# A decoder layer with an expert gather on one core: a new order ahead of the first gather, a planned share of the sums, and the gate multiply moved to ScalarE

## The reference, cut to what matters

```python
z = x @ w_in                      # split into [pool | q | k | v | gate_pool | gate_attn]
m = sigmoid(g_pool) * (pool_out @ w_up_pool) + sigmoid(g_attn) * (attn_out @ w_up_attn)
x = layer_norm(ALPHA * x + m @ w_out)                       # layer norm 1
def peer(xb):                                               # a block of 128 tokens
    q = (xb @ w_query).reshape(128, 8, 2, 128)
    sc = einsum('thcd,hcnd->thcn', q, sub_keys)             # 8 heads, two halves, 128 keys each
    ...                                                     # product-key top 16 of 128*128 experts
    gate = softmax(best_s)                                  # [128, 8, 16]
    u = take(expert_u, idx); h = gelu(einsum('td,thkd->thk', xb, u))
    return einsum('thk,thkd->td', gate * h, take(expert_v, idx))
x = layer_norm(ALPHA * x + peer(x))                         # layer norm 2
```

## Time and profile before

| | us |
|---|---|
| median of 3 runs | 3237.91 (3232.53 to 3238.44) |
| the profiled execution | 3230.01 |
| its span, from the first to the last instruction | 3228.2 |
| TensorE clock granted, mean | 0.929 of full |
| busy: PE / DVE / ACT / POOL | 2623.8 / 2404.6 / 687.4 / 1262.6 |
| DMA | 1258.54 MB, mean 390 GB/s |

### The profile page before, as it was taken

How to read it: one execution, slowest core, us unless ns; L and a number is a source line. 1 busy time by engine, 2 the same in 40 slices (tenths; PEclk the granted TensorE clock), 3 DMA queues, 4 the chain that set the end, 5 groups by cost and what they waited for, 6 DMA issues and landing times.

```text
span 3228.2 us, 28882 instructions
## 1 busy us (share of the span) xinstructions
PE 2623.8 (81%) x7884; PEld 1407.8 (44%) x7884; DVE 2404.6 (74%) x5540; ACT 687.4 (21%) x2001; POOL 1262.6 (39%) x1060
## 2 busy tenths in 40 slices
PE   8789999889898978889889898988666667666766
PEld 7776566555454534444344454443222222222222
DVE  2178666999967667898887667788999996666666
ACT  2123312222231121221332112221211121111111
POOL 0022343334443433334334343433445445444543
PEclk9899999999999989999999999999888888888898
DMA  6899999999999989999999999999999999999997
GB/s 200 234 385 368 354 412 386 408 368 406 413 420 416 420 358 414 420 399 413 358 348 379 419 420 405 408 405 383 376 418 419 420 382 422 421 421 422 421 422 330
DMA packets 204215, 1258.54 MB, mean 390 GB/s; under 512 B 31132, under 2 KB 34796, under 8 KB 68496
## 3 DMA queue, kind: packets, MB, share of 16 engines
q0 software_dynamic: 152064, 1107.36, 84.3%
q1 hardware_dynamic: 49376, 143.45, 12.2%
q10 hardware_dynamic: 2616, 5.88, 0.5%
HBM read 1250.93 MB, written 5.79 MB: 389 GB/s over the span
## 4 chain that ended last, share of the span: by engine, by line
PE 39%; DVE 26%; DMA 23%; issue 4%; DVEq 3%; ACT 3%; POOL 1%; SPq 0%; ACTq 0%; POOLq 0%
DMA ring<-in_uv,idx 21%; PE acc L890 20%; PE wide L873 11%; DVE ring L1139 10%; DVEq L1125 3%; DVE acc_v L1149 3%; PE wide L1047 3%; PE wide L1069 2%; ACT diag L689 1%; DMA wring<-in_w_q 1%; DVE hw L1144 1%; PE wide L981 1%; PE wide L963 1%; DVE ipart L1456 1%; DVE big L1448 1%
## 5 line engine op out<-in xcount | busy, mean ns | idle before, releaser
L890 PE MATMUL acc<-ring,diag 128*128 128x512 f32 (+1 forms) x3168 | 1637.2, 662 | 547.0 <-ACT diag L689 546.3
L652 POOL DMA_INDIRECT ring<-in_uv,idx x1056 | 1262.4, 1195 | 1939.1 <-PE acc L890 1558.6
L1139 DVE CUSTOM_DVE_ANT_0 ring<-ring,xb 128x1024 f32<-128x1024 f32 x1056 | 1269.7, 1223 | 356.4 <-DMA ring<-in_uv,idx 354.9
L890 PEld LDWEIGHTS acc<-ring,diag 128*128 128x128 f32 (+1 forms) x3168 | 631.5, 208 | 1411.7 <-issue 1391.8
L873 PE MATMUL wide<-xm,wring 128*128 128x256 f32 (+5 forms) x2624 | 638.0, 394 | 20.5 <-DMA wring<-in_w_q 16.5
L873 PEld LDWEIGHTS wide<-xm,wring 128*128 128x128 f32 x2624 | 462.1, 195 | 219.7 <-issue 98.0
L679 ACT ACTIVATE hgelu<-hdot 128x2 f32<-128x2 f32 x528 | 107.1, 203 | 1453.5 <-DVE hdot L1139 1452.9
L689 ACT ACTIVATE diag<-ident,hw 128x128 f32<-128x128 f32 x768 | 279.2, 395 | 539.6 <-DVE hw L1144 539.1
L1149 DVE SCALAR_TENSOR_TENSOR acc_v<-ring,hw,acc_v 128x1024 f32<-128x1024 f32 x264 | 339.3, 1285 | 27.0 <-issue 2.6
L1144 DVE TENSOR_TENSOR hw<-hgelu,gate 128x2 f32<-128x2 f32 x528 | 85.0, 161 | 122.3 <-ACT hgelu L679 104.4
L1069 PE MATMUL wide<-wring,big 128*128 128x256 f32 (+1 forms) x576 | 131.1, 380 | 1.1 <-DVE big L1332 1.1
(11 more groups left out here) (190 smaller groups left out, 1265.4 us busy)
## 6 DMA issues: line engine op xcount, KB each, us to landing
wring<-in_w_a SPq DMA_DIRECT2D x168, 512.0 KB, 7.7
wring<-in_w_q SPq DMA_DIRECT2D x64, 576.0 KB, 8.2
ring<-in_uv,idx POOLq DMA_INDIRECT x1056, 12.6
xb<-in_x_rows SPq DMA_DIRECT2D x8, 512.0 KB, 12.6
out_y_prompt<-xb ACTq DMA_DIRECT2D x8, 512.0 KB, 8.3
att<-in_ln_g SPq DMA_DIRECT2D x4, 512.0 KB, 8.2
att<-in_ln_b SPq DMA_DIRECT2D x4, 512.0 KB, 11.6
xm<-in_xT SPq DMA_DIRECT2D x1, 1536.0 KB, 11.5
```

Source lines behind the costliest of these rows:

```text
L652: pool.indirect_dma_start(ring[:, s % RING, :], None, uv, bass.IndirectOffsetOnAxis(ap=idx[:, n % ROWS, j:j + 1], axis=0))\
L890: k = mm(acc[0:width, c * 512:(c + 1) * 512], diag[:, r % DIAGS, 0:width], ring[:, s % RING, D + c * 512:D + (c + 1) * 512], start=(s == f ...
L1139: V.tensor_tensor_reduce(u, u, x, 1.0, 0.0, ALU.mult, ALU.add, hdot[:, k, j:j + 1])\
```

## The change

There are three parts.

1. **The order in front of the first gather, and some places in the other groups.** `store_states()` is called after the load of gate unit 6 instead of after the last unit of `w_out`. The pool mixer's product of group 0 goes to other PSUM banks (`mix_banks`) and stands after the twelfth gate unit. The sample attention's last product stands behind `w_out`. The first unit of `w_out` waits for half the merged channels only. The table `FIRST_ATTENTION` has other numbers. In groups 1 to 3 some ACT evacuations stand 0.3 to 0.5 of a batch later, and group 1's plan ends 3 batches earlier.
2. **The table of sums.** `ON_DVE`, before the second slot of every second batch, comes from `plan_sums()`, which adds up estimated costs of PE and DVE for each batch and gives a batch's second slot to DVE where its estimate says so. Summed by DVE in each of the nine peer parts, in order of time (the sixth is the samples): before 32, 32, 32, 32, 32, 8, 32, 32, 32, in all 264; now 42, 15, 33, 25, 48, 7, 1, 24, 31, in all 226. PE sums the rest, 792 before and 830 now. In the second part the first 40 batches give DVE none.
3. **The gate multiply.** DVE's `tensor_tensor` on `hw` is gone. ACT multiplies each slot's gelu by its gate with one ACTIVATE (a copy scaled by a column of `gate`) for each slot, between two drains, and builds the diagonals right after, at the place of the gelu instead of 0.99 of a batch later. ACT now waits for `gate_ready` at the first batch that uses a new softmax. DVE waits for `w_ready` only in front of its own sums, and four batches back, before `hdot` is written again. Some softmaxes are made for all 8 heads at once: 16 of them instead of 20.

In this order: the table of sums, SP's place of the stores, ACT's `experts()`, the sample attention's last product on PE, and DVE's `experts()`.

```diff
+def plan_sums():
+    batches = BATCH0[-1]
+    pe, dve, pace = [0.0] * batches, [0.0] * batches, [5.1] * batches
...
+            pe_done = max(pe_done, now) + sum(pe[k] for k in near) / len(near) + 1.8
+            dve_done = max(dve_done, now) + sum(dve[k] for k in near) / len(near) + 2.8
+            if max(pe_done + 1.8, dve_done + 1.3) < now + pace[m]:
+                on_dve = m % 2 == 1
+            else:
+                on_dve = dve_done + 1.3 < pe_done + 1.8
...
-                    if g == 0 and pos == POS_OUT + N_OUT - 1:
+                    if g == 0 and pos == POS_GATE + 6:
                         store_states()
...
                         act.wait_ge(dot_done, BATCH * (m + 1))
-                        nc.scalar.activation(hgelu[:, k, :], hdot[:, k, :], ACT.Gelu).then_inc(gelu_done, 1)
-                        yield m + 0.99
-                        act.wait_ge(w_ready, m + 1)
+                        at = BATCH * m - SLOT0[n]
+                        for e, (peer, a, _, _) in enumerate(GATES):
+                            if peer == n and a * TOPK == at:
+                                act.wait_ge(gate_ready, e + 1)
+                        nc.scalar.activation(hgelu[:, k, :], hdot[:, k, :], ACT.Gelu)
+                        act.drain()
+                        for j in range(BATCH):
+                            w = nc.scalar.activation(hw[:, k, j:j + 1], hgelu[:, k, j:j + 1], copy,
+                                                     scale=gate[:, n % ROWS, at + j:at + j + 1])
+                        w.then_inc(w_ready, 1)
+                        act.drain()
                         for j in range(BATCH):
                             s = BATCH * m + j
                             if on_dve(s):
...
-                yield CLOCKS[0].attention(count, 0.9)
+                yield CLOCKS[0].norm() + 0.1
                 pe.wait_ge(s_pt_evac, 2)
...
+                        if m >= SMALL:
+                            dve.wait_ge(w_ready, m - SMALL + 1)
...
                         yield m + 0.98
-                        at = BATCH * m - SLOT0[n]
-                        dve.wait_ge(gelu_done, m + 1)
-                        V.tensor_tensor(hw[:, k, :], hgelu[:, k, :], gate[:, n % ROWS, at:at + BATCH], ALU.mult)\
-                            .then_inc(w_ready, 1)
                         s = BATCH * m + BATCH - 1
                         if on_dve(s):
+                            dve.wait_ge(w_ready, m + 1)
                             fence()
```

More of the change, by code:

```diff
@@ L310, in gate_area, with on_dve, pe_slots, dve_slots @@
     return n * gate_width(g)
+ON_DVE = plan_sums()
+PE_SLOTS = list(accumulate(1 - x for x in ON_DVE))
+DVE_SLOTS = list(accumulate(1 * x for x in ON_DVE))
+def on_dve(s):
+    return ON_DVE[s]
+def pe_slots(s):
+    return PE_SLOTS[s]
+def dve_slots(s):
+    return DVE_SLOTS[s]
 def scores_before(g, c):
@@ L504, in gates, with mix_banks @@
             return big[:, gate_area(g, c):gate_area(g, c) + gate_width(g)]
+        def mix_banks(g):
+            if g == 0:
+                return [wide[0][:, 512 + c * P:512 + (c + 1) * P] for c in range(4)]
+            n = cols(g) - c0_of(g)
+            return [ps[:, 0:n] for ps in (pj[0], pj[1], wide[1][:, 0:512], wide[1][:, 512:1024])]
         def up_banks(k):
@@ L1000, in sample_attention @@
                 m.then_inc(s_score, 1)
-                yield CLOCKS[0].attention(count, 0.7)
+                yield CLOCKS[0].attention(count, 0.63)
                 pe.wait_ge(s_p, 1)
@@ L1056, in merged @@
                     for b in joined(g):
+                        if k == 0 and b == 1:
+                            hold(pe, m_ready, g * N_UP + N_UP)
                         m = out(g, k, b)
@@ L1298, in sample_attention @@
                 mx, nm, den, sk = sSmall[:, 0:2], sSmall[:, 2:4], sSmall[:, 4:6], sSmall[:, 6:8]
-                yield CLOCKS[0].attention(count, 0.15)
+                yield CLOCKS[0].attention(count, 0.13)
                 dve.wait_ge(s_score, 1)
@@ L1310, in sample_attention @@
                 V.tensor_tensor(sk, sSink, mx, ALU.subtract).then_inc(s_max, 1)
-                yield CLOCKS[0].attention(count, 0.55)
+                yield CLOCKS[0].attention(count, 0.5)
                 dve.wait_ge(s_exp, 1)
```

156 lines of the change are left out of this document (105 added, 51 removed).

## The result

The changed kernel takes 3190.05 us (median; 3184.95 to 3196.80), the kernel before in the same comparison 3235.22: a ratio of 0.9859, 95% interval 0.9842 to 0.9877. Won were 45 us; 83 were forecast. The profiled execution has a span of 3190.3 us.

What follows compares the result with a forecast made beforehand. Transfers at 422 GB/s were taken as the pace, held back by PE in the first block and DVE from 2244 us. 12 + 20 + 51 = 83 us off 3230 gave 3147, plus 4 made 3151; forecast 3115 to 3195, range 3092 to 3222.

Steps and rivals of the forecast that it cites:

- Front: Before the first gather: `w_query` 10, attention product 4.6, scores 2, stores -5; about 12 us won (0 to 20).
- 12.5 and 9.3 us: In front, the chain's waits for `w_query`: 12.5 us for the first unit, 9.3 us for the later wait at 171.
- The later wait for `w_query`: In front, a 9.3 us wait at 171 us that competes with nine gathers and may shrink; left in.
- First block: In the first block's part, ten sums fewer on PE win 20 us, bounds 0 and 36.
- PE sets the pace: In the first block's part PE, busy 409 of 436 us, holds the transfers back.
- Rest: Behind the first block, by stretch: 5, 5, 20, 6 and 15 us; 51 us won in all, bounds 0 and 109.
- Here DVE was the limit: From 2244 to 2899 us, 100 us off DVE's 549 win 15 of 22 us.
- PE's sums: Sums at 2.07 us each: 48 more behind the first block add 99 us to PE; 81 from 2244 to 2899.
- ACT: Over the run, two ACTIVATEs and two drains cost 0.6 us a batch, 317 us, bringing ACT to 1004 us.
- Rival 3: Over the run, ACT holds everybody: each batch on the chain pays 0.6 us; slower, 3305 with half of them; chance 0.10.
- Rival 2: Behind the first block, PE takes DVE's place, so the 51 us do not come: 3198 us; chance 0.17.
- The signs: Whole run: first gather before 160 us, tenth before 195, first block about 415, DVE under 480, ACT near 1000.

Runs made afterwards that it cites:

- e12: e10 with nine k and v stores one by one from gate unit 6 on, four pool-state stores behind the fourth `w_query` load: 3170.6 us, ratio 0.9811.
- e7: Kernel before with the planned table of sums and the multiply on ACT, old order: 3187.5 us, ratio 0.9851.
- e3: Kernel before with the gate multiply on ACT alone, old order and old table: 3201.3 us, ratio 0.9899.
- e8: Changed kernel with PE multiplying only the first 512 of 1024 columns of nearly every slot it sums: 3161.5 us, ratio 0.9776.
- e10: Changed kernel with the new order in front only, groups 1 to 3 at old places (earlier `w_out` start kept), e7's table: 3170.4 us, ratio 0.9810.
- e9: Changed kernel with ACT's two multiplies of each batch made twice, first into an unread place: 3200.4 us, ratio 0.9893.
- e11: e10 with all 13 early stores one by one behind the units from gate unit 6 on: 3178.3 us, ratio 0.9824.

## Why the prediction was right in direction and too large

The time lies in the range, 5 us from the forecast's slow end, with 45 of the 83 us. By the traces it is 38 (7.7 + 8.2 + 22). The other 7 are that the profiled run of the kernel before lay 5 us under its median, where the prediction added 4 for this, and the changed kernel's 2 us over its own.

- **Front: 12 forecast, 9.6 at the first gather, 7.7 at the tenth.** Read as PE's idle time, the terms came out nearly as forecast: the wait at the first `w_query` unit went from 10.2 to 1.2 us (10 forecast), the 4.8 us at the transposes were filled by the product (4.6), the 5.4 in front of the scores became 3.0 (2), and the stores cost 5.4 (5). The unit behind the stores also ran slower, 3.55 us against the 1.79 that one took before, at a granted clock of 0.66 from 75 to 80 us. The prediction took its 12.5 and 9.3 us from pieces of the chain, and the 13.05 us there now are such a piece too; it is not what the stores cost. The step that failed is "The later wait for `w_query` (9.3 us at 171) competes with nine gathers and may shrink; I leave it in": PE's waits for those units between the first and the tenth gather grew from 6.1 to 8.8 us, and 1.9 of the 9.6 us were gone at the tenth. So the place to measure a gain in front is the tenth gather: e12 won 10 us at the first and nothing at the tenth.
- **First block: 20 forecast from ten sums fewer on PE, 8.2 measured.** "PE sets the pace" failed. PE is busy 22 us less there, as the forecast had it, but the table gave nothing (e7 against e3), and half of all PE's sums only 5 us (e8). The multiply gave 14, which the prediction had not counted in this stretch, and the new places took 6 back. That some gain came here is luck: none of it is from the step that was forecast.
- **Rest: 51 forecast, 22 measured.** By stretch against the forecast: 3.8 (5), 6.5 (5), 6.4 (20). From the fourth block's end to the last block's end 5.2 were won, where 21 were forecast. In the fourth block the multiply alone won 12 (e3), and the order's places for the later groups, which the prediction did not cost at all, took 10 (e10 against the changed kernel). With old places the fourth block wins 16.7 and the whole kernel 64 of the 83 us. Behind it "Here DVE was the limit" failed: DVE is busy 61 us less from the samples' end on (100 forecast, with the multiplies' idle time counted as busy), and that stretch is 5 us shorter. What limits it now was not tried.
- **PE's sums** were priced too high. 38 more in all at 2.07 us would be 79 us; they took 16 (1653.3 - 1637.2). From the samples' end on PE does nothing else, and 924 matmuls take 464 us where 768 took 434, at a granted clock of 0.93 instead of 0.86: 30 us more, where 81 were forecast. What raised the clock was not tried.
- **ACT.** Forecast 317 us more, measured 261 busy (948.8 - 687.4), the pair of multiplies 0.48 us. The estimate from the Trainium skill's price list ("ScalarE: Activation LUTs", What ACT_TABLE_LOAD costs) was 0.47, and the trace agrees. With the two drains, which do not count as busy, the 0.6 us a batch came true: in the batch shown above the gelu ends at 706.97 us and the diagonals start at 707.60. Rival 3 falls: twice the multiplies cost 10 us (e9).
  The skill's rule that the multiply belongs on VectorE (the same page, Rules for kernel authors) did not pay in this kernel: one multiply for both columns is shorter there, 161 ns against two of 289, yet the part that moved it to ACT won 32 us alone (e3).
- **Rival 2** (PE takes DVE's place, 3198) came nearest in time, but for another reason than it named. It had 99 us more of PE eat the gain of the later blocks; but where PE's sums fell away (e8), the second and third block won 0.5 and 1.3 us.
- **The signs.** The first gather before 160 us, no PE gap of 10 us at `w_query`, diagonals that no longer wait for DVE, ACT near 1000 us (949): right. The first block's part of 415 us (420), the tenth gather before 195 (197.35), DVE under 480 (488) and 418 GB/s there (414): just missed. None of the signs against the forecast came: PE's wait for diagonals fell to 445 us, PE is at most 93% busy in a stretch, and the gate units waited 5.4 us for weights, not 12.

What sets the first block's pace now, with PE at 92%, DVE at 80% and 392 GB/s, is not shown. That instructions waiting at the head of a list do it is argued from e8 and e10 only.

## What to carry to other kernels

A short instruction between two engines is priced by where it stands in a list, not by its length: try it on the engine that has its input, even if it is slower there. Parts of a change are not additive (alone, order and table lost 4 and 12 us and the multiply won 32, in sum some 16 won; together they won 45), and a split of work that is planned for another dependency can cost time until that dependency is gone (the table: 12 us lost alone, 14 won with the multiply), so time each part with and without the others. A part that only "reorders" has a cost wherever it applies, not only where it was meant to help; and a gain ahead of a pipeline is read where the pipeline first refills, not where it starts. A transfer's piece of the chain runs from issue to landing; what it costs an engine is that engine's idle time in its own timeline (13.05 and 5.41 us here).

## What the runs showed of the hardware

- Four stores of 128 x 8 x 15 numbers held the DMA engines for some 10 us. In e12 SP issues them from 122.5 to 128.2 us and nothing more until 134.9; from 130 to 135 us the DMA engines were over 100% busy (1.65) at 14 GB/s. Nine stores of k and v states, one behind each unit, cost PE nothing that its trace shows: from 60 to 85 us it was busy all the time (e11).
- Units of 576 KB that shared the DMA engines with gathers arrived 3.9 us apart, at 409 GB/s in all (e12).
- With half of the sums left out, the granted clock's mean fell from 0.946 to 0.821 of 2.4 GHz, though PE stayed busy for 70% of the span (e8).
